# DeltaNet decays from cumulative sums made once, and one-row broadcasts of them in place of the decay products on TensorE

## The reference, cut to what matters

```python
gc = jnp.cumsum(g, axis=-1)                      # g: log decay of a token, a head, a direction
decay = jnp.exp(jnp.where(incl, gc[..., :, None] - gc[..., None, :], -jnp.inf))
a_mat = jnp.where(strict, jnp.einsum('bhnid,bhnjd->bhnij', kb, k) * decay, 0.0) + eye
sol = lax.linalg.triangular_solve(a_mat, rhs, left_side=True, lower=True, unit_diagonal=True)
qk = jnp.einsum('bhnid,bhnjd->bhnij', q, k) * decay
...
v_new = u_i - w_i @ s
o_i = (q_i * jnp.exp(g_i)[..., None]) @ s + qk_i @ v_new
s = s * jnp.exp(g_last)[..., None] + (k_i * jnp.exp(g_last - g_i)[..., None]).T @ v_new
```

## Time and profile before

| | us |
|---|---|
| median of 3 runs | 2906.47 |
| lowest and highest | 2906.46, 2907.76 |
| the profiled execution | 2908.57 |
| its span | 2907.0 |
| TensorE busy | 2775.2 (95%) |
| VectorE busy | 1862.4 (64%) |
| ScalarE busy | 1374.1 (47%) |
| GpSimd busy | 621.0 (21%) |

### The profile page before, as it was taken

How to read it: one execution, slowest core, us unless ns; L and a number is a source line. 1 busy time by engine, 2 the same in 40 slices (tenths; PEclk the granted TensorE clock), 3 DMA queues, 4 the chain that set the end, 5 groups by cost and what they waited for, 6 DMA issues and landing times. The chain is left out here.

```text
span 2907.0 us, 51741 instructions
## 1 busy us (share of the span) xinstructions
PE 2775.2 (95%) x17261; PEld 2685.4 (92%) x17261; DVE 1862.4 (64%) x3027; ACT 1374.1 (47%) x2265; POOL 621.0 (21%) x772
## 2 busy tenths in 40 slices
PE   6889999999897899999999999999999999989997
PEld 6889999999896899999999999999999999979997
DVE  5778998899635466576566656656655665754433
ACT  2134343333335355556556555555655655554332
POOL 4122223222111013113112311311321231130010
PEclk9999999999998899999999999999999999999998
DMA  8766667666532422222212212222221222132432
GB/s 291 255 230 234 236 236 242 236 232 243 202 124 72 145 69 71 70 65 76 72 61 74 78 58 70 78 70 69 72 72 61 74 78 89 68 130 98 140 123 94
DMA packets 101313, 367.70 MB, mean 126 GB/s; under 512 B 12496, under 2 KB 14560, under 8 KB 100368
## 3 DMA queue, kind: packets, MB, share of 16 engines
q1 hardware_dynamic: 69408, 252.74, 25.4%
q0 software_dynamic: 24512, 97.51, 9.9%
q10 hardware_dynamic: 7344, 16.80, 1.6%
HBM read 348.51 MB, written 18.48 MB: 126 GB/s over the span
## 5 line engine op out<-in xcount | busy, mean ns | idle before, releaser
L476 PE MATMUL bank<-h_hi,w_hi 128*128 128x384 f32 x2832 | 1054.7, 372 | 28.4 <-DVE h_lo L1197 12.9
L478 PE MATMUL bank<-h_hi,w_lo 128*128 128x384 f32 x2832 | 958.9, 339 | 0.0
L477 PE MATMUL bank<-h_lo,w_hi 128*128 128x384 f32 x2832 | 955.7, 337 | 0.0
L439 DVE TENSOR_TENSOR w_lo<-raw,w_hi 128x1024 fp32r<-128x1024 f32 x418 | 556.7, 1333 | 418.9 <-ACT w_hi L431 407.5
L431 ACT ACTIVATE w_hi<-raw 128x1024 fp32r<-128x1024 f32 x418 | 442.5, 1060 | 412.3 <-PE bank L478 389.4
L476 PEld LDWEIGHTS bank<-h_hi,w_hi 128*128 128x128 f32 x2832 | 540.3, 191 | 48.1 <-issue 31.9
L477 PEld LDWEIGHTS bank<-h_lo,w_hi 128*128 128x128 f32 x2832 | 541.0, 191 | 14.4 <-issue 7.7
L478 PEld LDWEIGHTS bank<-h_hi,w_lo 128*128 128x128 f32 x2832 | 536.4, 189 | 0.0
L1129 DVE SCALAR_TENSOR_TENSOR ada_terms<-raw_ada,cond_rows 128x1024 f32<-128x1024 f32 x256 | 316.6, 1237 | 14.5 <-DMA raw_ada<-in_late 9.0
L1563 POOL TENSOR_TENSOR qk_sq<-conv 128x386 f32<-128x386 f32 x32 | 26.0, 831 | 941.3 <-PE bank L757 908.0
L476 PE MATMUL bank<-y_hi,w_hi 128*128 128x384 f32 x512 | 173.8, 340 | 7.5 <-DVE y_lo L1256 4.9
(11 more groups left out here) (237 smaller groups left out, 4407.9 us busy)
## 6 DMA issues: line engine op xcount, KB each, us to landing
raw<-in_stream SPq DMA_DIRECT2D x482, 512.0 KB, 3.3
raw_ada<-in_late POOLq DMA_DIRECT2D x128, 512.0 KB, 3.9
y_kept<-y POOLq DMA_DIRECT2D x15, 384.0 KB, 2.9
bias<-in_bias POOLq DMA_DIRECT2D x16, 256.0 KB, 2.9
S<-in_state ACTq DMA_DIRECT2D x16, 256.0 KB, 2.6
out_state_out<-s_out ACTq DMA_DIRECT2D x16, 256.0 KB, 2.0
y<-in_x ACTq DMA_DIRECT2D x1, 3072.0 KB, 20.0
y<-in_x POOLq DMA_DIRECT2D x1, 3072.0 KB, 10.2
```

Of the source, the lines that this page charges most:

```text
L439: nc.vector.tensor_tensor(w_lo[:, mk % SPLIT_SLOTS, :], raw[:, raw_n % RAW_SLOTS, :], w_hi[:, mk % SPLIT_SLOTS, :].bitcast(F32), ALU.subtr ...
L476: nc.tensor.matmul(bank[:, 0:T], w_hi[:, slot, w], hi[:, kt, :], start=kt == 0, stop=False)
L477: nc.tensor.matmul(bank[:, 0:T], w_hi[:, slot, w], lo[:, kt, :], start=False, stop=False)
L478: last = nc.tensor.matmul(bank[:, 0:T], w_lo[:, slot, w], hi[:, kt, :], start=False, stop=kt == KT - 1)
```

## The change

The cumulative sums of g are made once, in `ba`, in two forms. Token on the partition: the sums that the table is made of anyway are copied over g in `bg` (VectorE, `fallen`). Token along the row: six new products (`rows`) of g with the masks, a copy on ScalarE, and a store to `gc_rows` in HBM. In each turn ScalarE loads the four rows (u) of the next head for all three chunks, repeated on all 128 partitions, into rows 4 to 7 of `y` (`fall`, 6 KB a partition, so 768 KB). It does so at `values 1`, and for head 0 in `dnP` at part (4, 1). The decay argument is then row minus the partition's sum, at most 0: 12 operations of GpSimd at the `decay` items. ScalarE takes the exps from there and from `fall`. The decay and broad products are gone from TensorE, and five of the 84 ring products with them. VectorE's `g_now` moves from `squares` to the start of the turn, GpSimd's gate copy from the start of the turn to `values 0`, and in `dnE` the load of rows 10 to 15 from the start to `unit`, with the last two `psplit` behind 10 parts.

```diff
-_chain = [(5, ("norms",)), (2.5, ("decay", 0)), (2, ("decay", 1)), (1.5, ("broad", 1)), (0, ("unit",)), (2, ("decay", 2)),
-          (1.5, ("broad", 2)), (1, ("gram", 0)), (2, ("gram", 1)), (2, ("gram", 2)), (1, ("values", 0)),
-          (1, ("values", 1))]
+_chain = [(3, ("norms",)), (0, ("decay", 0)), (0, ("broad", 1)), (0, ("decay", 1)), (0, ("broad", 2)), (0, ("decay", 2)),
+          (0, ("unit",)), (13, ("gram", 0)), (2, ("gram", 1)), (2, ("gram", 2)), (1, ("values", 0)), (1, ("values", 1))]
...
 def last_plan():
-    plan = [("psplit", n) for n in range(len(FIRST_ROWS))] + merge(_chain, OUT_PARTS[:OUT_BESIDE])
+    early, late = [item for _, item in _chain[:7]], [(1, _chain[7][1])] + _chain[8:]
+    loaded = sum(rows for _, rows, row in FIRST_ROWS if row >= 8)
+    plan = [("psplit", n) for n in range(3)] + early + OUT_PARTS[:loaded] + [("psplit", n) for n in range(3, 5)]
+    plan += merge(late, OUT_PARTS[loaded:OUT_BESIDE])
...
-        if what == "decay":
-            made.append((f"decay{arg}", "act"))
-        elif what == "broad":
-            made.append((f"broad{arg}", "act"))
-        elif what == "norms":
+        if what == "norms":
             made += [("ss0", "act"), ("ss1", "act")]
...
-        g_mask = [inv["c", c] for c in range(CHUNKS)]
+        fall = y[:, 4:8, :].rearrange("p r t -> p (r t)").rearrange("p (c u i) -> p c u i", c=CHUNKS, u=4)
...
         def ring_free(name):
 
             n = PRODUCT_AT[name] - RING
+            turn_before = n < 0
+            if turn_before:
+                n = max(m for m in range(len(PRODUCTS)) if m % RING == n % RING)
             before, reader = PRODUCTS[n]
-            return reader, "v_newB" if before == "applyB" else before, n < 0
+            return reader, "v_newB" if before == "applyB" else before, turn_before
 
...
+                for c in range(CHUNKS):
+                    for d, mask in enumerate(("le", "ge")):
+                        mm = nc.tensor.matmul(banks[6][32 * d:32 * d + 32, c * P:(c + 1) * P], bg[:, c, 64 + 32 * d:96 + 32 * d],
+                                              K[mask], start=True, stop=True)
+                done("pe", "rows", mm)
 
...
                         multiply(pe, phase, turn, arg, item[2], h_hi, h_lo)
-                    elif what == "decay":
-                        wait_steps(pe, turn, ("pool", f"g_mask{arg}", True), ring_free(f"decay{arg}"))
-                        for d, mask in enumerate(("gt", "lt")):
-                            mm = nc.tensor.matmul(ring(f"decay{arg}")[:, 2 * d * P:(2 * d + 2) * P], K[mask],
-                                                  g_mask[arg][:, 2 * d:2 * d + 2, :].rearrange("p v i -> p (v i)"),
-                                                  start=True, stop=True)
-                        done("pe", f"decay{arg}", mm)
-                    elif what == "broad":
-                        wait_steps(pe, turn, ring_free(f"broad{arg}"))
-                        mm = nc.tensor.matmul(ring(f"broad{arg}")[:], K["ones"],
-                                              g_mask[arg][:].rearrange("p v i -> p (v i)"), start=True, stop=True)
-                        done("pe", f"broad{arg}", mm)
...
+                act.dma_start(dram["gc_rows"].rearrange("c r t -> r c t"), bt2[0:64, :].rearrange("r (c t) -> r c t", c=CHUNKS))\
+                    .then_inc(s["rows_out"], 16)
                 for n, dst in enumerate((neg_egc, beta_egl, egl)):
                     wait_steps(act, turn, ("pe", f"sums{n}"))
                     done("act", f"table{n}", nc.scalar.activation(dst[:].rearrange("p c d h -> p (c d h)"),
...
+
+                def load_fall():
+                    rows = dram["gc_rows"].rearrange("c (d r) t -> (c d) r t", d=2)[:, bass.ds(2 * next_head, 2), :]
+                    act.dma_start(fall.rearrange("p c (d v) t -> p (c d) v t", d=2), rows.unsqueeze(0).broadcast_to([P, 2 * CHUNKS, 2, P]))\
+                        .then_inc(s["fall_in"], 16)
+
...
+                    if item == ("part", 4, 1) and phase == "dnP":
+                        act.wait_ge(s["rows_out"], 16)
+                        act.wait_ge(s["x_out"], 16)
+                        load_fall()
...
 
-                        wait_steps(act, turn, ("pe", f"decay{arg}"), ("pe", "outB", 1))
-                        done("act", f"decay{arg}", nc.scalar.activation(decay[arg][:].rearrange("p u i -> p (u i)"),
-                                                                        ring(f"decay{arg}")[:], ACT.Exp))
+                        wait_steps(act, turn, ("pool", f"fallen{arg}"))
+                        wide = decay[arg][:].rearrange("p u i -> p (u i)")
+                        done("act", f"decay{arg}", nc.scalar.activation(wide, wide, ACT.Exp))
                     elif what == "broad":
-                        wait_steps(act, turn, ("pe", f"broad{arg}"))
+                        act.wait_ge(s["fall_in"], 16 * (turn + HEADS_BEFORE[phase] + 1))
+                        wait_steps(act, turn, ("pe", "outB", 1))
                         done("act", f"broad{arg}", nc.scalar.activation(q_dec[arg][:].rearrange("p u i -> p (u i)"),
-                                                                        ring(f"broad{arg}")[:], ACT.Exp))
+                                                                        fall[:, arg].rearrange("p u i -> p (u i)"), ACT.Exp))
...
+                        if arg == 1 and next_head is not None:
+                            wait_steps(act, turn, ("pool", f"fallen{CHUNKS - 1}"), ("act", "broad2"))
+                            load_fall()
...
-                wait_steps(dve, turn, ("act", "table1"), ("dve", "bg"))
+                wait_steps(dve, turn, ("pe", "sums2"), ("dve", "bg"), ("act", "table0"))
+                done("dve", "fallen", nc.vector.tensor_copy(bg[:, :, 64:P], banks[3][:, 0:CHUNKS * 2 * DN_V_HEADS]
+                                                            .rearrange("p (c h) -> p c h", c=CHUNKS)))
+                wait_steps(dve, turn, ("act", "table1"))
...
+                    wait_steps(dve, turn, ("pool", f"fallen{CHUNKS - 1}", True))
+                    done("dve", "g_now", nc.vector.tensor_copy(
+                        g_now[:], bg[:, :, 64:P].rearrange("p c (d h) -> p c d h", d=2)[:, :, :, bass.ds(2 * head, 2)]))
...
-                    elif what == "squares" and next_head is not None:
-
-                        wait_steps(dve, turn, ("pool", "g_mask2", True))
-                        done("dve", "g_now", nc.vector.tensor_copy(
-                            g_now[:], bg[:, :, 64:P].rearrange("p c (d h) -> p c d h", d=2)[:, :, :,
-                                                                                           bass.ds(2 * next_head, 2)]))
...
-                        wait_steps(dve, turn, ("dve", f"gram{c}"), ("act", f"decay{c}"), ("pe", f"broad{max(c, 1)}"),
-                                   ("pe", "applyB", True))
+                        wait_steps(dve, turn, ("dve", f"gram{c}"), ("act", f"decay{c}"), ("pe", "applyB", True))
...
 
-            def mask_steps(pool, turn, *which):
-
-                for c in range(CHUNKS):
-                    wait_steps(pool, turn, ("dve", "g_now"), *which)
-                    lone()
-                    for u in range(4):
-                        d, v = u // 2, u % 2
-                        i = nc.gpsimd.tensor_scalar(g_mask[c][:, u, :], K["le" if d == 0 else "ge"],
-                                                    g_now[:, c, d, v:v + 1], 1.0, ALU.mult, ALU.mult)
-                    done("pool", f"g_mask{c}", i)
-
             def dn(pool, phase, turn):
                 head, _ = heads(phase, turn)
                 gated = y[:, 2:4, :]
                 if phase == "dn1":
                     lone()
                     pool.dma_start(y[:, 8:18, :], dram["y_kept"][:, 0:10, :]).then_inc(s["first_in"], 16)
-                if phase in ("dn0", "dn1"):
-                    pool.wait_ge(s["x_out"], 16)
-                    tile_read(pool, phase, turn, -1)
-                    lone()
-                    done("pool", "gate_now", nc.gpsimd.tensor_copy(gated, y[:, 0:2, :]))
-                elif phase == "dnE":
+                if phase == "dnE":
                     gated = y[:, 0:2, :]
-                    lone()
-                    pool.dma_start(y[:, 2:8, :], dram["y_kept"][:, 10:16, :]).then_inc(s["first_in"], 16)
                 for item in DN_PLANS[phase]:
                     what, arg = item[0], item[1] if len(item) > 1 else None
                     if what == "squares" and phase != "dnE":
 
                         square_qk(pool, turn, ("pe", "applyB"))
-                        mask_steps(pool, turn, ("pe", "applyB"))
+                    elif what == "decay":
+
+                        c = arg
+                        pool.wait_ge(s["fall_in"], 16 * (turn + HEADS_BEFORE[phase] + 1))
+                        wait_steps(pool, turn, ("dve", "g_now"), ("pe", "outB", True))
```

(32 more changed lines are left out.)

## The result

The changed kernel takes 3012.9 us (median of 4 runs, 3009.7 to 3014.5) against 2906.95 of the kernel before (median of 4): a ratio of 1.036, with a 95% interval from 1.0345 to 1.0381. The profiled executions have spans of 3011.4 and 2907.0 us, 104.4 apart. The prediction said slower, but by 29 us, and its range ended at 2960.

The account below looks back on a forecast made before the run. TensorE sets most of the turn, a VectorE chain its first third. Terms +35.0 + 0.6 + 3.1 - 9.4 + 0 = +29.3 us gave 2935.8 us, 1.0% slower; range 2895 to 2960, likeliest case 2919 to 2949.

Parts of the forecast that it names:

- None of the 4.3 us is a gain unless the chain's start moves: Repeated turn: TensorE's removed decay and broad blocks, 4.3 us a turn, save nothing because VectorE's chain starts no earlier.
- The chain: Store of y, GpSimd's twelve, third decay, split, gram 0: forecast to lengthen each of 14 turns by 2.5 us, +35.0.
- 12 operations of the old ones' form and size, so 4.21 us: GpSimd's decay arguments at the turn's start: assumed to take as long as the twelve old mask operations.
- The prediction's own formula: Steps from `fallen` through decay2 and the split to VectorE's gram 0: 1138.1 against 1136.52, before contention.
- the hold-up by `unit`, 0.9 us: VectorE's `unit` amid GpSimd's twelve: stalls delay `fallen2` by 0.9 us, between 0 and 1.2.
- The third rival: Clock falls in each turn: 1 to 3 us a turn, +14 to +42, middle 2964; sign, 0.52 us matmuls; 12%.
- Single places: Terms outside the repeated turns: after `ba` +3.1, first head turn -9.4, `dn1` +0.6, last head turn 0.
- The products of the rows: After `ba`: six new products take 2.6 us, a VectorE copy adds 0.5, so dnP starts 3.1 us later.
- the first turn's own term: First head turn: gram 0 at 1024.6 instead of 1033.99, 9.4 us earlier, ends 6 and 10.
- `dn1` and `dnE`: `dn1`: a load issued ahead of `fallen`, +0.6 us; `dnE`, the last head turn: 0, ends -2 and +4.
- GpSimd's last load: In `dnE`: the kept rows' load waits for `broad2` and `fallen2`, 5.9 us later, with 10 parts to run meanwhile.
- the 1.6 us of the forecast: Repeated turn: gram 0 late by 1.6 us a turn before any contention on GpSimd.

Follow-up runs that it names:

- e7_vector: Changed kernel with the twelve decay-argument operations moved from GpSimd to VectorE, ScalarE's order and the plan kept; 2923.2 us.
- e8_both: Changed kernel with the twelve operations on VectorE, decay and broad items six parts later behind part 8's split, gram 0's weight 6.5; 2862.0 us, ratio 0.985.
- e1_mult: Changed kernel with GpSimd's twelve operations as multiply, multiply (factor 0) instead of subtract, min; 2959.9 us.
- e3_order: Changed kernel with decay and broad items planned six parts later, behind part 8's split, the twelve operations still on GpSimd; 2958.2 us.
- e4_plan: Changed kernel with the plan weight ahead of gram 0 at 12.5 instead of 13, so the sum is 91.5; 2992.3 us.
- e5_submul: Changed kernel with GpSimd's twelve operations as subtract, multiply instead of subtract, min; 3012.7 us.
- e2_const: Changed kernel with GpSimd's twelve subtract, min operations reading a constant mask instead of the loaded rows; 3017.4 us.

## Why the prediction was half right

**Right: the bound and the chain.** "None of the 4.3 us is a gain unless the chain's start moves" is shown by e7_vector, and the other way round by e8_both, where gram 0 comes 2.7 us earlier and the turn is 2.7 us shorter. The chain (store, twelve operations, third decay, split, gram 0) is shown by the three periods that come out to 0.1 us from GpSimd's time alone.

**Wrong: the price of the twelve.** The step that failed is "12 operations of the old ones' form and size, so 4.21 us". Form and size were the same; the pair of ALU operations wasn't. The prediction's own formula with 8.50 in place of 4.21, and without the 0.9 for contention, gives 1.6 + 4.3 = 5.9 us up to gram 0; measured are 5.98. No row of before had such a pair on GpSimd, so this was an unknown price, and it should have stood in the sum with an upper end of its own.

**Wrong: the hold-up by `unit`, 0.9 us.** In the changed kernel one of the twelve takes 0.91 us instead of 0.71 while `unit` runs, so 0.2 us in all. In e1_mult's second turn, where the operations are short, three of them take 0.47, 0.65 and 0.53 instead of 0.37: 0.5 us. The rule of the Trainium skill that I weighed there ("SBUF — State Buffer", on the two separate sides) would have each stand still for the other. Rows agree for `w_lo` behind GpSimd's `inv_d` (2.31 us, like the earlier trace rows), and for one of the twelve that starts behind `w_lo` in e3_order's second turn:

```profile
1126.70 1.22 DVE L436 TENSOR_TENSOR w_lo<-raw,w_hi 128x1024 fp32r<-128x1024 f32 x1
1126.83 1.67 POOL L1597 TENSOR_SCALAR decay<-y,g_now 128x128 f32<-128x128 f32 x1
```

It takes 1.67 us instead of 0.71 and ends after `w_lo` does. They don't for `unit`: its four short operations start while one of the twelve is running and take 1.25 us in all, where they took 1.16 alone. So the size of the stall depended on which operations met.

**Missed: the plan's weight.** I followed the work moved in front of gram 0 and not what 92 instead of 91.5 does to the positions behind it: a wait of 1.0 us in each of 14 turns, and 1.3 us of each period by e4_plan.

**Partly right: the clock.** The third rival's sign, matmuls of 0.52 us inside the turns, is there. The clock does fall to its 1.2 GHz level (granted clock 0.50) in the turn, after a wait of 5.3 us, and in e7_vector after one of 2.40 us, in 9 of the 14 turns that have it. But what follows waits for VectorE's chain anyway: from gram 0 to `p2` are 13.56 us instead of 13.33. So in the changed kernel the rival's mechanism came and its price, 1 to 3 us a turn, didn't. Where the clock fell later in the turn, behind the wait for `inv_d`, the price was 3.0 to 3.5 us (single turns of five of the experiments).

**Single places.** The products of the rows took 1.5 us, not 2.6, and dnP starts 1.8 later than before, not 3.1. The first turn's gram 0 is 4.5 earlier. With dnP's 1.8 taken out, the first turn's own term is -6.3, where the sum had -9.4: the twelve take 9.39 us there. In e5_submul and e2_const, which are alike up to there and have the same price, its mark lies at 1028.0 and 1032.6, so one profile resolves this term to a few us at best. `dn1` and `dnE` cost 3.2 + 1.4 where I had 0.6 in all. GpSimd's last load is issued behind `fallen2`, as forecast, but that wasn't free: in `dnE` TensorE waits for the split rows (`h_lo`) twice, 5.7 and 10.5 us, where it waited once, 7.0 us.

With measured terms the prediction's sum is 14 x 7.45 - 4.5 + 3.2 + 1.4 = 104.4 us, where it had 29.3. That is an account of the marks and no test; the tests are the runs above. No run joins e1_mult's operations with e4_plan's weight, so it isn't shown that the two together leave only the 1.6 us of the forecast.

## What to carry to other kernels

Take the duration of an instruction from a row with the same ALU operations, not only the same engine, opcode and shape. Where there is no such row, the price is unknown and needs its own upper bound, above all if the instruction goes onto the path that sets the end. Work taken off a busy engine pays only as far as the chain that meets it moves too: here 69 us of matmuls bought nothing until the split went ahead of the decays, and the same idea then gave 1.5%.

## What the hardware showed unexpectedly

GpSimd's `tensor_scalar` on 128x128 fp32 took 0.37 us for multiply and multiply, 0.52 for a lone minimum with a constant, and 0.71 for each of subtract-min, subtract-multiply, add-min and multiply-min, with no effect of the source tile. With non-zero results the multiplications stay at 0.37 us but start 0.45 us apart instead of 0.35. VectorE did subtract-min on the same tiles in 0.27 to 0.29 us each, but for one of the twelve: it took 1.07 us in e7_vector's second turn (1124.06 to 1125.13), while GpSimd's product of y (1124.02 to 1125.05) was running. Whether the low price belongs to multiplications in general, and not only to this pair in this program, these runs don't show.
